# Five start offsets in place of one for the raw and low weights of the paired feed-forward units

## What is computed

```python
for l in range(DEPTH):
    x = _layer_norm(DN_ALPHA * x + 0.5 * _swiglu(x, ffn1_w_gate[l], ffn1_w_up[l], ffn1_w_down[l]), ln1_g[l], ln1_b[l])
    mix = _hybrid_mixer(x, ...)      # three branches: latent attention, mLSTM, retention; gates, output projection
    x = _layer_norm(DN_ALPHA * x + mix, ln2_g[l], ln2_b[l])
    x = _layer_norm(DN_ALPHA * x + 0.5 * _swiglu(x, ffn2_w_gate[l], ffn2_w_up[l], ffn2_w_down[l]), ln3_g[l], ln3_b[l])

def _swiglu(x, w_gate, w_up, w_down):
    return (jax.nn.silu(x @ w_gate) * (x @ w_up)) @ w_down
```

## Time and profile before

| | |
|---|---|
| median of 3 runs | 1296.79 us (1296.75 to 1297.57) |
| span of the profiled execution | 1294.6 us, granted clock 0.999 |
| TensorE matmul busy | 1282.7 us (99%) |
| TensorE weight load busy | 1161.9 us (90%) |
| VectorE busy | 890.3 us (69%) |
| ScalarE busy | 637.9 us (49%) |
| loads on SP's queue | 231.8 MB, 55.9% of 16 engines |

### The profile page before, as it was taken

How to read it: one execution, slowest core, us unless ns; L and a number is a source line. 1 busy time by engine, 2 the same in 40 slices (tenths; PEclk the granted TensorE clock), 3 DMA queues, 4 the chain that set the end, 5 groups by cost and what they waited for, 6 DMA issues and landing times.

```text
span 1294.6 us, 18958 instructions
## 1 busy us (share of the span) xinstructions
PE 1282.7 (99%) x8177; PEld 1161.9 (90%) x8177; DVE 890.3 (69%) x1086; ACT 637.9 (49%) x654; POOL 71.2 (5%) x59
## 2 busy tenths in 40 slices
PE   8999999999999999999999999999999999999998
PEld 8888889998999998888898888899989998988886
DVE  6666667998675676656676666779977766766655
ACT  5444446684634444444454444466736444544441
POOL 0399000000000000000000000000000000000000
PEclk9999999999999999999999999999999999999999
DMA  8755547543566555556556555466436565555562
GB/s 296 233 188 188 194 145 222 186 131 101 193 195 196 171 174 182 191 195 195 166 192 195 188 187 189 153 196 196 131 98 207 184 196 163 191 188 187 187 193 95
DMA packets 176243, 234.83 MB, mean 181 GB/s; under 512 B 7904, under 2 KB 146784, under 8 KB 176032
## 3 DMA queue, kind: packets, MB, share of 16 engines
q1 hardware_dynamic: 175776, 231.78, 55.9%
q0 software_dynamic: 240, 1.71, 0.4%
q10 hardware_dynamic: 144, 0.13, 0.1%
HBM read 232.56 MB, written 1.05 MB: 180 GB/s over the span
## 4 chain that ended last, share of the span: by engine, by line
PE 98%; DVE 1%; ACT 1%; DMA 0%; DVEq 0%; issue 0%
PE ps L1474 22%; PE ps L1449 21%; PE ps L1457 11%; PE ps L1377 11%; PE ps L1375 11%; PE ps L1376 11%; PE ps L1440 5%; PE ps L1397 1%; PE ps L1409 1%; PE ps L1671 1%; PE ps L1630 0%; PE ps L1631 0%; ACT rot_sw L626 0%; PE ps L1657 0%; PE ps L1658 0%; PE ps L1656 0%
## 5 line engine op out<-in xcount | busy, mean ns | idle before, releaser
L831 DVE TENSOR_TENSOR wlo<-raw,whi 128x2048 fp32r<-128x2048 f32 (+1 forms) x218 | 492.5, 2276 | 197.8 <-ACT whi L540 197.7
L540 ACT ACTIVATE whi<-raw 128x2048 fp32r<-128x2048 f32 (+1 forms) x218 | 413.5, 1898 | 293.3 <-DMA raw<-w_in 112.6
L1449 PE MATMUL ps<-xpair,whi 128*128 128x512 f32 x1216 | 290.1, 390 | 0.0
L1449 PEld LDWEIGHTS ps<-xpair,whi 128*128 128x128 f32 x1216 | 225.4, 188 | 45.0
L1375 PE MATMUL ps<-xpair,whi 128*128 128x256 f32 x800 | 224.3, 280 | 0.0
L1377 PE MATMUL ps<-xpair,wlo 128*128 128x256 f32 x800 | 222.7, 278 | 0.0
L1376 PE MATMUL ps<-xpair,whi 128*128 128x256 f32 x800 | 222.6, 278 | 0.0
L1457 PEld LDWEIGHTS ps<-xpair,wlo 128*128 128x128 f32 x1216 | 154.5, 189 | 6.1
L1457 PE MATMUL ps<-xpair,wlo 128*128 128x256 f32 x1216 | 156.4, 281 | 0.0
L1376 PEld LDWEIGHTS ps<-xpair,whi 128*128 128x128 f32 x800 | 150.7, 188 | 0.4
L1375 PEld LDWEIGHTS ps<-xpair,whi 128*128 128x128 f32 x800 | 150.1, 188 | 0.4
(11 more groups left out here) (234 smaller groups left out, 1617.0 us busy)
## 6 DMA issues: line engine op xcount, KB each, us to landing
raw<-w_in SPq DMA_DIRECT2D x60, 1024.0 KB, 5.2
raw<-ffn_w_down SPq DMA_DIRECT2D x44, 1024.0 KB, 4.9
raw<-ffn_w_gate SPq DMA_DIRECT2D x43, 1024.0 KB, 5.3
raw<-ffn_w_up SPq DMA_DIRECT2D x43, 1024.0 KB, 5.3
raw<-w_br SPq DMA_DIRECT2D x12, 1024.0 KB, 5.0
raw<-w_out SPq DMA_DIRECT2D x8, 1024.0 KB, 4.8
raw<-mla_w_uq SPq DMA_DIRECT2D x4, 576.0 KB, 3.9
raw<-mla_w_ukv SPq DMA_DIRECT2D x2, 1024.0 KB, 4.9
```

Of the source, the lines that this page charges most:

```text
L540: act.activation(unit(whi, n), unit(raw, n), ACT.Copy).then_inc(w_hi, 1)
L831: dve.tensor_tensor(w_low(n), unit(raw, n), unit(whi, n).bitcast(F32), ALU.subtract).then_inc(w_lo, 1)
L1449: pe.matmul(ps[:, bank, :], wh[:, kk, cols], xpair[:, kk, :, :], start=kk == 0, stop=kk == KC - 1, skip_group_check=True)
```

## The change

In `unit`, a paired unit's raw and low tile begins n % RING * SHIFT floats into its slot: 0, 64, 128, 192 or 256 bytes in slots 0 to 4, in place of 128 bytes in all. The slot's pitch leaves 256 bytes beyond the unit, so the last one ends where the next slot begins. The high tile stays where it is, as do all units that are not paired.

```diff
         if ring is whi:
             at_n = n % RING * UNIT + shift_of(n) + lo
         else:
-            at_n = n % RING * PITCH + (2 * SHIFT if is_paired(n) else shift_of(n)) + lo
+            at_n = n % RING * PITCH + (n % RING * SHIFT if is_paired(n) else shift_of(n)) + lo
         return ring[:, at_n:at_n + (size or size_of(n))]
```

## The result

The changed kernel takes 1299.12 us, against 1297.01 us for the kernel before in the same rounds, 20 runs of each. The ratio is 1.0015, 95% interval 1.0009 to 1.0021: slower by 0.15%, or 2.1 us. That is clear of noise, and above the range of the prediction, which ended at 1298.4. One of the 20 runs of the changed kernel took 1597.92 us at a granted clock of 0.753; it is left out of the ratio and doesn't move the median.

What follows compares the result with a forecast made beforehand. The prediction took TensorE, 98% of the chain, to bound the kernel. Its three terms, 0 + 0 + 0, on the 1294.6 us execution plus 2.2 us outside the span gave 1296.8 us, range 1295.2 to 1298.4.

Steps and rivals of the forecast that it cites:

- Parts 2 and 3: VectorE and ScalarE (L831 moves at most 12 ns, L540 24) and loads (slot 1 0.2 us sooner): 0 on the path.
- Part 1: TensorE's reads of the low tile, the only part on the path: the new starts leave its cadence alone, term 0.
- the slower rival: At L1457 low weights meet the input at a worse step: 1298.8 us at 2 ns a matmul, 1302.9 at 6; chance 0.07.
- The sign that the prediction gave for this rival: For the slower rival: L1457's median or most over 284 ns.
- The bounds of part 1: Low runs: 5.8 us less if every moved run is quick, 6.1 us more at 6 ns a moved matmul.
- the rival's threshold: The slower rival decides from 2.5 ns a matmul (2.6 us / 1024), only if it hits all four slots.
- The quick rival: Low runs at some new start take 114 ns a matmul: 1295.4 us for one slot, 1291.0 for four; chance 0.10.
- Faster by over 0.2%, within it, slower: Chances for the whole time: 0.08 faster by over 0.2%, 0.87 within (0.83 no change, 0.02 and 0.02), 0.05 slower.

Runs made afterwards that it cites:

- e4: Kernel before with the low run's weights read from the high tile (0 modulo 512), all else in place: 1299.01 us against 1297.00, ratio 1.0017.
- e1: Kernel before with all paired units 64 bytes into their slot, raw and low tiles at 0 modulo 256: 1299.69 us against 1297.00, ratio 1.0022.
- e8: Kernel before with input tile xpair and the paired raw and low tiles both 64 bytes lower: 1305.16 us in a single run.
- e13: Kernel before with a spare 64-byte line ahead of the ring, so weights, input and all later tiles stand higher: 1296.71 us against 1296.92, ratio 0.9997.
- e14: As e13, but the low tiles stay at 64 modulo 256, against the kernel before: 1299.27 us against 1296.92, ratio 1.0020.
- e7: Kernel before with only the input tile xpair 64 bytes lower, weights staying at 64 modulo 256: 1311.62 us in a single run.

## Why the prediction was wrong

- What bounds the kernel, right: TensorE at 98% of the chain, no new wait, before and after.
- Parts 2 and 3, right: L831 and L540 as before, and nothing of SP's queue on the path. The loads of slot 1's paired units even land in 5.10 us (median of 16) where they took 5.35. That TensorE alone is slowed is shown by e4, where nothing but its read changed.
- **Part 1, the step that failed**: the term was set to 0, "since the earlier trace rows are the same instructions or the same widths at three starts modulo 512". It is 1.9 us by the trace (26 to 34 ns for each of 64 units), and 2.1 by the medians. Starts of 64 and 320 modulo 512 are one place modulo 256, so the earlier trace rows hold one place and not two. The earlier trace rows have only whi at 0, with the low weights still at 64, in a triple of three reads, and can't stand for a run of 16 low tiles; the same unit in e1, with the low tile at 0 too, is 0.1 us longer. With these two gone no row spoke for a cost of 0 at starts of 0, 128 and 192 modulo 256. The prediction knew this of 128 and 192, and took 0 as shown. The nearest row that did bear on it was named in the slower rival and set aside: L1440's median of 283 where both operands begin at 0 modulo 256. That is also the median of e1, though at L1440 the weights' tile is the moving operand, so it was a hint and not a proof. The sign that the prediction gave for this rival came: L1457's most is 288, over 284.
- The bounds of part 1, from -5.8 to +6.1 us, held the value, and so did the slower rival, at its lower price (2 ns a matmul, 1298.8 us). Its 1024 matmuls cost 1.9 ns each on average. Its place was half right: in slots 0 and 4 the low run is even 3 ns shorter, and the price of 36 ns is behind it, at L1449 of the next unit or L1474 of the down unit.
- The range ended at 1298.4, the price of 1.5 ns a matmul, on the strength of that zero. With the earlier trace rows read as one place, it would have had to go up to the whole 2.5 ns of the rival's threshold.
- The quick rival didn't come in any paired unit at any of the six places. It did in e8, with the input moved, so the low run can run at 114 ns; but there L1449 takes 6.8 us more over the whole span where L1457 takes 4.8 less.
- Faster by over 0.2%, within it, slower: 0.15% lies within, where 0.87 stood. That was luck: 0.83 of it stood for no change, and only 0.02 for a price under 2.5 ns a matmul, which is what came.

The Trainium skill (SBUF — State Buffer, section "Who interferes with whom") says that TensorE has separate read ports for moving operand and weights and never waits on anyone. By that, e13 and e14 would be equal. They are 2.6 us apart, and differ only in where the raw and low tiles lie against the others; e4 shows the same low run with no access of another engine moved. The measurement decides: the page's rule doesn't hold for the two reads of TensorE here, and no run here tests it for other engines.

## What to carry to other kernels

In this kernel, where TensorE is busy all the time, the place of the low weights modulo 256 bytes, against the tiles read with them, is worth up to 0.2% of the time, and the price may show in the next matmuls and not in those that read the tile. So measure the run after it as well, and try one place for all tiles first, at several starts: a sum over mixed places hides what each costs. Before a set of rows is taken for evidence over several addresses, reduce the addresses modulo every period in question: two that fall on one residue are one case.

## What the runs showed of the hardware

- At equal shapes a low run of 16 matmuls takes 1.878 us at 96, 1.884 at 192, 1.887 at 64, 1.892 at 32, 1.912 at 0 and 1.924 at 128 modulo 256, with the input at 0; the 15 wide matmuls behind it take 3.427, 3.463, 3.427, 3.447, 3.428 and 3.410. The two don't go together, and neither is graded by the distance. Places 256 bytes apart are the same to 1 ns.
- It is the relation that counts: everything from the ring on moved by 64 bytes gives 0.9997, all but the low tiles 1.0020. Whether it is the relation to the input, to the high weights or to both is open, as e14 and e7 point different ways.
- A stream of 256-column matmuls has two lasting cadences, 118 and 113 ns, at one and the same addresses; that the mixer's choice differs between executions of one program is inferred from their times. Why, and how to choose the quick one, stays open.
